# One gate step ahead of a retention group's scores, the outputs' transposes one tile later, and three sums moved in the second feed-forward group

## What is computed

```python
# retention, 8 heads (64 for q and k, 128 for v)
scores = einsum(qc, kc) * intra_decay
intra  = einsum(scores, vc);  cross = einsum(qc, q_from_start, s_prev)
ret = groupnorm(intra + cross) * ret_gn_g
ret = silu(g_r) * ret                       # g_r is a projection of h: the gate
# feed-forward
f = square(relu(h2 @ w_ff1)) @ w_ff2        # 1024 -> 4096 -> 1024
```

## Time and profile before

| | us |
|---|---|
| median of 3 runs | 1713.94 |
| the runs | 1712.99 to 1715.09 |
| the profiled execution, its own time | 1713.04 |
| its span (first to last instruction) | 1711.2 |
| TensorE busy | 1674.3 (98% of the span) |
| VectorE busy | 1007.6 (59%) |
| GpSimd busy | 709.6 (41%) |
| ScalarE busy | 607.1 (35%) |
| mean granted TensorE clock | 0.997 |

### The profile page before, as it was taken

One profiled execution on the slowest core, in us unless ns is written; L12 is line 12 of the kernel. 1 busy time (PEld: TensorE's weight loads), 2 busy tenths in 40 slices (PEclk: granted clock), 3 DMA queues, 4 the chain that ended last, 5 costly groups with the idle time before them and its releaser, 6 DMA issues.

```text
span 1711.2 us, 25635 instructions
## 1 busy us (share of the span) xinstructions
PE 1674.3 (98%) x9872; PEld 1395.5 (82%) x9872; DVE 1007.6 (59%) x1382; ACT 607.1 (35%) x1022; POOL 709.6 (41%) x299
## 2 busy tenths in 40 slices
PE   5999999999999999999999999999999999999998
PEld 5877877777989898988888999787888888888876
DVE  7766666786447464743121547699665748383736
ACT  5565666210111212121000256435353434435352
POOL 2011111253314141414444643573667585858550
PEclk9999999999999999999999999999999999999999
DMA  9011001264401010103111444635684755648272
GB/s 357 17 38 39 26 26 63 78 230 168 156 26 53 25 54 25 53 25 147 50 49 49 148 173 160 221 136 198 245 349 158 290 220 233 275 169 339 101 295 99
DMA packets 51877, 238.00 MB, mean 139 GB/s; under 512 B 6980, under 2 KB 7876, under 8 KB 45896
## 3 DMA queue, kind: packets, MB, share of 16 engines
q1 hardware_dynamic: 44240, 216.62, 33.6%
q10 hardware_dynamic: 7544, 20.08, 3.1%
HBM read 209.41 MB, written 27.28 MB: 138 GB/s over the span
## 4 chain that ended last, share of the span: by engine, by line
PE 90%; DVE 6%; ACT 2%; issue 1%; DMA 1%; POOL 0%; SPq 0%; POOLq 0%; DVEq 0%; ACTq 0%
PE ps L736 11%; PE ps L738 11%; PE ps L737 11%; PE ps L1112 6%; PE ps L1114 6%; PE ps L1113 6%; PE ps L1157 4%; PE ps L1156 4%; PE ps L1155 4%; PE ps L822 3%; PE ps L823 3%; PE ps L824 3%; PE ps L997 2%; PE ps L875 2%; DVE fs_f L2101 2%; PE ps L999 2%
## 5 line engine op out<-in xcount | busy, mean ns | idle before, releaser
L553 POOL TENSOR_TENSOR w_hi<-raw,zero 128x1024 fp32r<-128x1024 f32 x58 | 113.4, 1955 | 461.2 <-PE ps L738 267.8
L736 PE MATMUL ps<-w_hi,a_hi 128*128 128x256 f32 x768 | 219.2, 285 | 0.8 <-DVE a_lo L1996 0.6
L738 PE MATMUL ps<-w_hi,a_lo 128*128 128x256 f32 x768 | 215.7, 281 | 0.0
L737 PE MATMUL ps<-w_lo,a_hi 128*128 128x256 f32 x768 | 215.4, 281 | 0.0
L1112 PE MATMUL ps<-w_hi,f_hi 128*128 128x512 f32 x440 | 175.4, 399 | 4.3 <-issue 4.1
L1113 PE MATMUL ps<-w_lo,f_hi 128*128 128x512 f32 x440 | 174.9, 397 | 0.0
L1114 PE MATMUL ps<-w_hi,f_lo 128*128 128x512 f32 x440 | 174.8, 397 | 0.0
L555 POOL TENSOR_TENSOR w_lo<-raw,w_hi 128x1024 fp32r<-128x1024 f32 x58 | 146.3, 2523 | 4.6
L736 PEld LDWEIGHTS ps<-w_hi,a_hi 128*128 128x128 f32 x768 | 144.9, 189 | 2.2 <-issue 0.9
L737 PEld LDWEIGHTS ps<-w_lo,a_hi 128*128 128x128 f32 x768 | 144.9, 189 | 0.2
L738 PEld LDWEIGHTS ps<-w_hi,a_lo 128*128 128x128 f32 x768 | 144.7, 188 | 0.0
(11 more groups left out here) (275 smaller groups left out, 4071.5 us busy)
## 6 DMA issues: line engine op xcount, KB each, us to landing
ring<-ops SPq DMA_DIRECT2D x42, 2048.0 KB, 8.4
raw<-wstream SPq DMA_DIRECT2D x100, 512.0 KB, 3.2
ada_r<-ada_rows SPq DMA_DIRECT2D x32, 512.0 KB, 4.4
w<-wstream SPq DMA_DIRECT2D x32, 512.0 KB, 3.3
ada_s<-ada SPq DMA_DIRECT2D x7, 1024.0 KB, 16.9
w1s<-wstream SPq DMA_DIRECT2D x12, 512.0 KB, 9.7
m_dram<-m1s ACTq DMA_DIRECT2D x1, 4096.0 KB, 15.5
m<-m_dram ACTq DMA_DIRECT2D x1, 4096.0 KB, 12.5
```

The lines of the kernel that those rows point to most:

```text
L553: nc.gpsimd.tensor_tensor(w_hi[:, slot, part], raw[:, h, :], zero[:, 0:1].broadcast_to([P, RAW]), ALU.add).then_inc(w_split, 1)
L736: nc.tensor.matmul(outp, lh, rh, start=(k == 0), stop=False)
L737: nc.tensor.matmul(outp, lh, rl, start=False, stop=False)
L738: last = nc.tensor.matmul(outp, ll, rh, start=False, stop=(k == chunks - 1))
```

## The change

Three edits, and no operation more or less:

- In a retention group TensorE takes gate step 0 ahead of `scores(0)`, and every later step one place earlier, so that one step is left behind the last output where there were two. The step waits for ACT's copy of the fifth v tile (it frees the bank) and the weights.
- The outputs' transposes stand behind tiles 1, 2 and 3 of the next group's first piece; they stood behind tiles 0, 1 and 2. The last group's (`last_r`) stay.
- In the second feed-forward group `operand_sums(3, 0, 5)` and `(3, 5)` become `(3, 0, 8)` and `(3, 8)`: three more sums stand ahead of `f_low(P1)`, the first low part of a product.

```diff
--- before.py
+++ after.py
@@ -971,8 +971,8 @@
                     last.then_inc(qk_tr, 1)
 
                 def before(t):
-                    if g and t < 3:
-                        for u in ((0, 1), (2,), (3,))[t]:
+                    if g and 0 < t < 4:
+                        for u in ((0, 1), (2,), (3,))[t - 1]:
                             r_transposed(g - 1, u)
 
                 piece_N(n, sub, a_hi, a_lo, lambda t: None if t < 2 else (ev_dve, ev - 5 + t) if t < 6 else (ev_dve, ev + t - 5),
@@ -1000,8 +1000,10 @@
                         if k == KC - 1:
                             last.then_inc(gemm_done, 1)
 
+                pe.wait_ge(ev_act, ea + 5)
+                pe.wait_ge(w_split, 4 * (n + 2) + 4)
+                g_steps(0, 1)
                 pe.wait_ge(ev_act, ea + 8)
-                pe.wait_ge(w_split, 4 * (n + 2) + 4)
                 scores(0)
                 for i in range(T):
                     if i < T - 1:
@@ -1009,7 +1011,7 @@
                         if i:
                             pe.wait_ge(state_done, 7 * g + i)
                         nc.tensor.matmul(kv_bank, qk[:, i, P:2 * P], vr[:, i, :], start=True, stop=True).then_inc(kv_done, 1)
-                    g_steps(3 * i, 3 * i + 1)
+                    g_steps(3 * i + 1, 3 * i + 2)
                     pe.wait_ge(st_ready, 8 * g + i + 1)
                     if i:
                         pe.wait_ge(o_copied, 8 * g + i)
@@ -1025,7 +1027,7 @@
                     last.then_inc(o_done, 1)
                     if i < T - 1:
                         scores(i + 1)
-                    g_steps(3 * i + 1, 3 * i + 3)
+                    g_steps(3 * i + 2, min(3 * i + 4, 3 * T))
                 pe.wait_ge(o_copied, 8 * g + 8)
                 g_steps(3 * T, 4 * KC)
 
@@ -2163,12 +2165,12 @@
                     operand_sums(0, 5)
                     operand_sums(1)
                     operand_sums(2)
-                    operand_sums(3, 0, 5)
+                    operand_sums(3, 0, 8)
                 f_low(P1, a11)
                 if first:
                     second_gate_row()
                 else:
-                    operand_sums(3, 5)
+                    operand_sums(3, 8)
                 dve.wait_ge(ff_sq, 8 * g + (6 if first else 4))
                 V.tensor_tensor(a21, a11, a21, ALU.subtract).then_inc(ff_s, 1)
                 dve.wait_ge(ff_sq, 8 * g + (8 if first else 7))
```

## The result

The changed kernel takes **1720.04 us** (median of 8 runs, 1714.2 to 1722.51), the kernel before 1714.51 beside it (8 runs, 1712.99 to 1715.7). The ratio is 1.0028, with a 95% interval of 1.0019 to 1.0037: slower, where 1710.4 was forecast. The profiled execution took 1718.58 us with a span of 1716.8, 5.6 more than before. The runs of the changed kernel lie 8.3 us apart, those of before 2.7; one execution was profiled, so where the others differ from it isn't shown. Lines of the kernel behind the moved step count two more than before.

A forecast was written before the change was run, and what follows sets the result against it. TensorE, busy 98% of the span, was taken as the bound, gains lying in its waits and lowered clock. Retention 2.6 plus feed-forward 0.9 gave 3.5 us off 1713.94: 1710.4 us, with an 8-in-10 range of 1708.3 to 1712.0.

The forecast's parts named there:

- what a group's new end costs: Retention group's end, one step left behind the last output: new wait for ACT's copy `o_copied`, taken as 0.05 us a group.
- Retention, the step ahead of the scores: Gate step fills 0.62 us of TensorE idle ahead of the scores: 0.64 us a group, 2.6 us in four groups.
- Retention, the transposes one tile later: Outputs' transposes in retention: DVE's gating and rotations move later, but no tile waits; price 0.
- Feed-forward: Second feed-forward group, sums moved: P4 earlier after 2.4 us of idle, clock full, new 1.75 us wait at P5; 0.9 us gained.
- Rival 4: Retention: transposes push DVE so tile 6 waits in three groups, 2.2 us each; 3.1 us slower, 1717.0 us; 4%.
- The bounds 530.7 and 530.9: Retention, tile 6: DVE's last read of its bank by 530.7, tile beginning not before 530.9, so no wait.

The follow-up runs named there:

- e1: Kernel before with only the gate step moved ahead of the scores, transposes and sums as before: 1730.01 us, ratio 1.009.
- e12: Kernel before with only the gate step moved, GpSimd's group-end weights waiting for DVE's first gate eviction: 1712.11 us, ratio 0.9985.
- e4: Changed kernel, with GpSimd's weights at a group's end waiting for DVE's first gate eviction: 1711.82 us, ratio 0.9982 to the kernel before.
- e7: As e4, but with the outputs' transposes left where they were before: 1710.37 us, ratio 0.997 to the kernel before.
- e2: Kernel before with only the outputs' transposes moved one tile later: 1716.02 us, ratio 1.0005.
- e6: As e4, with GpSimd's low part for P3 also waiting for DVE's low part of P5: 1710.45 us, ratio 0.9975 to the kernel before.
- e3: Kernel before with only the three sums moved ahead of the first low part in the second feed-forward group: 1713.53 us, ratio 0.999.
- e8: As e3, with GpSimd's low part for P3 waiting for DVE's low part of P5: 1713.58 us, ratio 0.9987 to the kernel before.
- e9: As e7, with GpSimd's low part for P3 also waiting for DVE's low part of P5: 1710.17 us, ratio 0.9971 to the kernel before.
- e10: As e7, but GpSimd's weights behind first and third group released after 12 of 16 normalizations: 1722.28 us, ratio 1.0044 to the kernel before.
- e11: As e7, but GpSimd's weights behind first and third group released after 14 of 16 normalizations: 1710.09 us, ratio 0.9974 to the kernel before.

## Why the prediction was wrong

**The step that failed** is what a group's new end costs. Under "Retention, the step ahead of the scores" the sum has "minus what the new end costs" and puts only the wait for `o_copied` there, 0.05 us a group; that the gate now ends sooner against everything else costs nothing in it. The reason given for that 0 stands under "Retention, the transposes one tile later", in the sentence "The 0.7 us by which TensorE reaches the group sooner move the transposes, and DVE's gating behind them, together with the tiles." It took everything at a group's end to move together. The edit to the transposes isn't the fault: the loss is there without it (e1). Three things stand there: TensorE's gate (0.7 us sooner), the outputs and DVE's normalizations (in their place), and GpSimd's weights, which go with the gate. The last pair moved against each other. I looked at GpSimd's later pieces, near the rotations, and not at the ones that its release by the last gate tile starts. The row at 513.40, 2.02 us long for an operation that takes 0.34, was in the trace of before and said that the two had just begun to touch. Measured, the term put at nothing is 17.9 us with the step alone (e1 against e12) and 8.2 in the changed kernel (against e4).

- **The step ahead of the scores** (2.6 us): right with the collision gone. Idle filled, nothing at `o_copied`, 0.7 us a group, 2.8 us timed (e12).
- **The transposes** (0): too low also by themselves. The bounds 530.7 and 530.9 were worked out at the second group, and the third has over 3 us of standstill on DVE ahead of the rotations. About 1.5 us in the profile (e4 against e7) where the price was 0; timed alone, no difference from before that is clear of the noise (e2). Against the delayed normalizations they helped.
- **Feed-forward** (0.9 us): right in the changed kernel's profile, with its pause, P5's wait and its cause (e6: held, the wait is gone). Timed, e3 against before: 1.4 us, with an interval of 0.2 to 3.3. The clock behind a pause of 2.3 us is not one value; I had taken it as full, so that the size agrees is in part luck of the execution.
- **Rival 4** had the right sign, the right pair of engines (DVE pushed by GpSimd) and a price not far off (3.1 us slower; 4.8 by the ratio), but another place: tile 6 and the rotations. Its "against", that GpSimd stands between two pieces there, was true of that place. The wait came at tile 2, behind the evictions. It got 4% because I worked out one place where the engines could meet and not all of them.
- The range ended at 1712.0: it held no case in which retention lost anything. The one such case with a time of its own, rival 4, stood at 1717.0, outside it.

## What to carry to other kernels

When an instruction is moved past others on one engine, list for each semaphore it raises who is released by it, and for each of those what the other engine of a pair that block each other (here DVE and GpSimd) is doing at that moment, in the old and in the new place. An operation that is several times its usual length, alone at the end of a train, marks an edge: moving either side by less than the train's length can turn one long operation into four. And an order that is good in itself may need the third engine held: here one wait on GpSimd turned 0.28% slower into 0.2% faster (e4), and 0.3% with the transposes left where they were (e7).

## What was not expected of the hardware

- **Turns.** Where DVE and GpSimd both had operations queued, neither finished its train first: one normalization of 0.34 us went for each GpSimd operation of 1.9 to 2.4 us, so DVE's took 2.0 to 2.6 us each and GpSimd's kept their length.
- **A loop's jump back on DVE** had 3.11 us (before), 3.33 us (e2) and 4.49 us (e7) of standstill, at the same place between the second and third group, where the two other groups have 0.14. That the jump is its cause follows from the place alone; what it consists of was not tried.
- **The clock behind a pause of 2.3 us** was the lower level in e3, e8 and e9 and the upper one in the changed kernel, e4, e6, e7, e10 and e11. Behind 3.09 us in the changed kernel, and 3.7 to 3.8 us in e1 and e10, it was the lower one, at once or within 2 us. The fall need not be there when TensorE starts again: in e9 it came about 1.2 us behind P4's first matmul. What decides at 2.3 us stays open, and with it about 1.6 us of any one execution.
